# A two-block transformer in one kernel: inverse roots on sums packed into four column tiles, and a convolutional FFN with the gate unit first

## The reference, cut to what matters

```python
def rmsnorm(x, g):                       # rms_norm in the first block is the same
    x32 = x.astype(jnp.float32)
    y = x32 * lax.rsqrt(jnp.mean(x32 * x32, axis=-1, keepdims=True) + RMS_EPS)
    return (y * g.astype(jnp.float32)).astype(x.dtype)

# first block, twice: SEQ 512, D_MODEL 1024; norm, w_in (3584 columns), retention and differential
# attention (rms_norm per head of 64 on dq, dk), w_out; norm, gated FFN (D_FF 2816)

# second block: layer 0 neighbourhood attention (na), layer 1 sliding window (swa);
# layer 0 does the 512 positions and 256 of context, layer 1's FFN the 512 alone
h = modulate(rmsnorm(x, g_attn[i]), sh1, sc1)
q, k, v = attn_inputs(h, w_in, gq, gk, n_kv)               # rmsnorm per head of 64 on q and k
...
def conv_ffn(h, w_up, conv_w, conv_b, w_down):
    t = h.shape[1]
    u = h @ w_up
    u_p = jnp.pad(u, ((0, 0), (CONV_W // 2, CONV_W // 2), (0, 0)))
    u = sum(u_p[:, tap:tap + t] * conv_w[tap] for tap in range(CONV_W)) + conv_b
    a, g = jnp.split(u, 2, axis=-1)
    return (a * jax.nn.silu(g)) @ w_down
```

## Time and profile before

| | before |
|---|---|
| device time, median of 3 runs | 3473.67 us (3472.83 to 3476.34) |
| the profiled execution: its time, its span | 3476.96 us, 3475.2 us |
| PE busy | 3143.3 us (90%), 15176 matmuls |
| DVE busy | 1960.5 us (56%) |
| ACT busy | 1252.3 us (36%) |
| POOL busy | 1072.6 us (31%) |
| chain that ended last | PE 64%, DVE 14%, issue 13%, ACT 4%, POOL 2% |
| L578, main matmuls | 54% of the chain |
| L502, `w_lo` on POOL | 364 of 2618 ns on average |
| L953, `w_hi` on ACT | 364 of 1115 ns on average |
| L1497, head norms' reciprocal | 42, 4038 ns on average |

### The profile page before, as it was taken

How to read it: one execution, slowest core, us unless ns; L and a number is a source line. 1 busy time by engine, 2 the same in 40 slices (tenths; PEclk the granted TensorE clock), 3 DMA queues, 4 the chain that set the end, 5 groups by cost and what they waited for, 6 DMA issues and landing times.

```text
span 3475.2 us, 44398 instructions
## 1 busy us (share of the span) xinstructions
PE 3143.3 (90%) x15176; PEld 2406.6 (69%) x15176; DVE 1960.5 (56%) x2788; ACT 1252.3 (36%) x1801; POOL 1072.6 (31%) x468
## 2 busy tenths in 40 slices
PE   6997689998899679999899988999999798988998
PEld 4752368886672258888687666888888576766777
DVE  5537765455736875455672775552454477566273
ACT  3224444222232535222322762441232226545232
POOL 2320144444330034444223222222223230234343
PEclk9989799999998889999899998999999899999999
DMA  3330034343340024444111001121112120022222
GB/s 132 121 107 0 18 120 149 126 150 102 109 149 0 0 85 145 133 145 133 37 54 58 24 22 48 55 64 63 60 60 67 37 68 13 31 67 85 82 92 92
DMA packets 72775, 269.59 MB, mean 78 GB/s; under 512 B 7920, under 2 KB 8944, under 8 KB 72560
## 3 DMA queue, kind: packets, MB, share of 16 engines
q1 hardware_dynamic: 71024, 264.34, 24.0%
q10 hardware_dynamic: 1664, 4.11, 0.3%
HBM read 266.32 MB, written 2.10 MB: 77 GB/s over the span
## 4 chain that ended last, share of the span: by engine, by line
PE 64%; DVE 14%; issue 13%; ACT 4%; POOL 2%; DVEq 1%; ACTq 0%; DMA 0%; POOLq 0%
PE ps L578 54%; PE ps L668 2%; PE ps L678 2%; DVE conv_y L1588 2%; POOL w_lo L502 2%; DVE conv_y L1584 2%; DVE n_xn L1448 2%; PE ps L725 1%; DVE n_rstd L1435 1%; PE ps L808 1%; PE ps L787 1%; DVE s_s L1864 1%; PE ps L611 1%; PE ps L826 1%; PE ps L634 1%
## 5 line engine op out<-in xcount | busy, mean ns | idle before, releaser
L502 POOL TENSOR_TENSOR w_lo<-w_raw,w_hi 128x1024 fp32r<-128x1024 f32 (+1 forms) x364 | 952.6, 2618 | 1618.7 <-ACT w_hi L953 1618.7
L578 PE MATMUL ps<-h_hi,w_hi 128*128 128x512 f32 x3040 | 1059.1, 383 | 138.9 <-DVE h_lo L1462 84.0
L578 PE MATMUL ps<-h_hi,w_lo 128*128 128x512 f32 x3040 | 1034.9, 375 | 0.0
L578 PE MATMUL ps<-h_lo,w_hi 128*128 128x512 f32 x3040 | 1033.4, 374 | 0.0
L953 ACT ACTIVATE w_hi<-w_raw 128x1024 fp32r<-128x1024 f32 (+1 forms) x364 | 405.6, 1115 | 1091.1 <-PE ps L578 1083.7
L578 PEld LDWEIGHTS ps<-h_hi,w_hi 128*128 128x128 f32 x3040 | 539.6, 192 | 286.7 <-issue 99.9
L578 PEld LDWEIGHTS ps<-h_lo,w_hi 128*128 128x128 f32 x3040 | 537.7, 192 | 102.8 <-issue 6.3
L578 PEld LDWEIGHTS ps<-h_hi,w_lo 128*128 128x128 f32 x3040 | 537.7, 192 | 101.9
L1584 DVE TENSOR_SCALAR conv_y<-u_pad,small 128x770 f32<-128x770 f32 (+1 forms) x88 | 148.0, 1682 | 150.0 <-ACT u_pad L1108 150.0
L1542 DVE SCALAR_TENSOR_TENSOR xT<-ps,mod,xT 128x512 f32 (+1 forms) x72 | 45.4, 659 | 309.7 <-PE ps L578 309.7
L1588 DVE SCALAR_TENSOR_TENSOR conv_y<-u_pad,small,conv_y 128x770 f32<-128x770 f32 (+1 forms) x176 | 195.7, 1112 | 26.2 <-DVE conv_y L1584 6.7
(11 more groups left out here) (187 smaller groups left out, 3649.2 us busy)
## 6 DMA issues: line engine op xcount, KB each, us to landing
mod_w<-w_mod_dram SPq DMA_DIRECT2D x96, 512.0 KB, 3.7
w_raw<-w_gu_dram SPq DMA_DIRECT2D x88, 512.0 KB, 3.6
w_raw<-w_down_dram SPq DMA_DIRECT2D x64, 704.0 KB, 4.1
w_raw<-w_up_dram SPq DMA_DIRECT2D x88, 512.0 KB, 3.6
w_raw<-w_in_dram SPq DMA_DIRECT2D x56, 512.0 KB, 3.7
w_raw<-na_qkv_dram SPq DMA_DIRECT2D x24, 512.0 KB, 3.6
w_raw<-w_out_dram SPq DMA_DIRECT2D x16, 512.0 KB, 3.6
w_raw<-swa_qkv_dram SPq DMA_DIRECT2D x12, 512.0 KB, 3.6
```

The costliest lines, as they stand in the source:

```text
L502: pool.tensor_tensor(w_lo[par][:, 0:cols], w_raw[par][:, 0:cols], w_hi[par][:, 0:cols].bitcast(F32), ALU.subtract).then_inc(w_lo_ready, 1)
L578: last = pe.matmul(acc[par][:, to:to + n], w[par][:, k * P:k * P + P], r[:, k, frm:frm + n], start=begin, stop=end)
```

## The change

**Matrices.** `mats` has ten 128x128 matrices for five. In `PACK`, columns 0 and 1 are 1/64 over the first and the second 64 partitions, and column 32 is 1/1024; the other columns of a tile's 32 are zero. `SPREAD64` and `SPREAD128` have a one where the row of a packed mean meets the partitions that it is for.

**Packed sums.** `groups(T)` divides the columns into four groups: 128 each at T = 512, and windows of 256 at 768. PE multiplies each group into a column tile of 32 partitions of one PSUM bank (`n_packed` in bank 7; `hn_packed` in banks 6 and 7 by parity), by four matmuls with a semaphore increment each where there was one (or two) over the whole array. Root and reciprocal then run over 128 or 256 columns in `n_rs` or `hn_rs`. Four more matmuls over 64 rows each spread the result to 128 partitions and T columns in `sums[0]` (banks 4 and 5), from which DVE's products read it; PE waits for the reciprocal before them. This holds for the eight norms and for the 42 head norms. The norms inside retention and attention (reciprocals at L1698 and L1757, 16 in all) are as before.

**Order in the `normed` phases.** The sum of a unit stands one unit later, and its spreading (`head_cast`) another unit later. The sum and the spreading of the last two units (`tail`) go behind K tiles 2 and 5 of the next phase's first unit; for swa the rotations beside it move by three places (`ROPE_AT`). DVE's loop becomes take, invert, scale, take, invert, scale.

**Conv.** The weights and the taps' table are put in the other order, so that the gate unit comes first. ACT copies a unit once three taps of the parity's previous use are done; Silu follows the taps of both; the product goes to a buffer of its own, `conv_z`. ACT makes the high part of f-1 behind its first copy of f, DVE the low part of f-1 between the two groups of taps. The first pair is peeled on ACT and DVE; the last high and low part stand behind the loop.

The diff, cut to its core:

```diff
+def groups(T):
+    if T == S:
+        return [(g, g * P, P, S * (g // 2) + P * (g % 2), 0, P) for g in (0, 2, 1, 3)]
+    return [(0, 0, 2 * P, 0, 0, 2 * P), (2, S, 2 * P, S, 0, P),
+            (1, 2 * P, 2 * P, 2 * P, 0, 2 * P), (3, S, 2 * P, S + P, P, P)]
...
+            def pack(to, select, square, T, begin=True, end=True):
+                return [pe.matmul(to[32 * g:32 * g + 32, 0:w], mats[:, PACK, select:select + 32],
+                                  square[:, frm:frm + w], start=begin, stop=end) for g, frm, w, _, _, _ in groups(T)]
+            def spread(select, r, T):
+                return [pe.matmul(sums[0][:, to:to + w], mats[g // 2 * HD:g // 2 * HD + HD, select + g % 2, :],
+                                  r[g // 2 * HD:g // 2 * HD + HD, frm:frm + w], start=True, stop=True)
+                        for g, _, _, to, frm, w in groups(T)]
...
             def head_sum(ph, n, par):
                 pe.wait_ge(hn_sq_ready, n + (ph["hn0"] + 1))
-                for to, _, w, _ in segments(ph["T"]):
-                    last = pe.matmul(sums[par][:, to:to + w], mat(MEAN64), hn_sq[par][:, to:to + w],
-                                     start=True, stop=True)
-                last.then_inc(hn_sum, 1)
+                for mm in pack(hn_packed[par], 0, hn_sq[par], ph["T"]):
+                    mm.then_inc(hn_sum, 1)
+
+            def head_cast(ph, n, par):
+
+                pe.wait_ge(hn_recip, n + (ph["hn0"] + 1))
+                if not isinstance(n, int) or n + ph["hn0"] > 0:
+                    pe.wait_ge(hn_out, n + ph["hn0"])
+                for mm in spread(SPREAD64, hn_rs[par], ph["T"]):
+                    mm.then_inc(hn_cast, 1)
...
+                def pair(i):
+                    unit(ph, i, 0, False)
+                    head_sum(ph, i * 2 - 1, 1)
+                    head_cast(ph, i * 2 - 2, 0)
+                    unit(ph, i, 1, False)
+                    head_sum(ph, i * 2, 0)
+                    head_cast(ph, i * 2 - 1, 1)
+
+                if n > 2:
+                    pair(1)
+                    with pe.Fori(2, n // 2) as i:
+                        pair(i)
+
+                def tail(k):
+                    if k == 2:
+                        head_sum(ph, n - 1, 1)
+                        head_cast(ph, n - 2, 0)
+                    if k == 5:
+                        head_cast(ph, n - 1, 1)
+                ends[0] = tail
...
+                    pack(n_packed, 32, n_sum_sq, T, True, False)
                     pe.wait_ge(n_sq_ready, KT * n0 + KT)
-                    add_up(n_sq[1], False, True).then_inc(n_sum, 1)
+                    for mm in pack(n_packed, 32, n_sq[1], T, False, True):
+                        mm.then_inc(n_sum, 1)
+                pe.wait_ge(n_recip, n0 + 1)
+                for mm in spread(SPREAD128, n_rs, T):
+                    mm.then_inc(n_cast, 1)
...
+                def hi(f):
+                    act.wait_ge(conv_step, BEGUN + f * 7 + (7 * n0 + 7))
+                    act.activation(a_hi[:, dyn(f), 0:W], row(conv_z[:, 0:W]), ACT.Copy).then_inc(conv_hi, 1)
+
                 def body(f, split):
+                    first = isinstance(f, int) and f == 0
                     for par in range(2):
                         act.wait_ge(mm_done, f * 2 + (ph["unit0"] + par + 1))
                         split(par)
-                        act.wait_ge(conv_step, BEGUN + f * 7 + 7 * n0)
+                        act.wait_ge(conv_step, BEGUN + 7 * n0 if first else BEGUN + f * 7 + (7 * n0 + 3 * par - 4))
                         for to, frm, n, _ in segments(T, CTX_AT):
                             last = act.activation(u_pad[par][:, 2 + frm:2 + frm + n], acc[par][:, to:to + n], ACT.Copy)
                         last.then_inc(acc_free, 1)
-                    act.wait_ge(conv_step, BEGUN + f * 7 + (7 * n0 + 6))
-                    act.activation(conv_y[1][:, 0:W], conv_y[1][:, 0:W], ACT.Silu).then_inc(conv_gate, 1)
-                    act.wait_ge(conv_step, BEGUN + f * 7 + (7 * n0 + 7))
-                    act.activation(a_hi[:, dyn(f), 0:W], row(conv_y[0][:, 0:W]), ACT.Copy).then_inc(conv_hi, 1)
-                units_of(ph, body)
+                        if par == 0 and not first:
+                            hi(f - 1)
+                    act.wait_ge(conv_step, BEGUN + f * 7 + (7 * n0 + 3))
+                    act.activation(conv_y[0][:, 0:W], conv_y[0][:, 0:W], ACT.Silu).then_inc(conv_gate, 1)
+                units_of(ph, body, peel=1)
+                hi(FH - 1)
...
+                        if T == S:
+                            last = dve.scalar_tensor_tensor(
+                                out=halves(row(n_xn[k % 4][:, 0:S])), in0=halves(row(xT[:, k, 0:S])), scalar=gain,
+                                in1=spread_out(T), op0=ALU.mult, op1=ALU.mult)
...
+                def invert(i, par):
+                    dve.wait_ge(hn_std, i * 2 + (h0 + par + 1))
+                    r = hn_rs[par][:, 0:packed(T)]
+                    dve.reciprocal(r, r).then_inc(hn_recip, 1)
+
                 def scale(i, par):
-                    dve.wait_ge(hn_std, i * 2 + (h0 + par + 1))
-                    dve.reciprocal(hn_r[par][:, 0:T], hn_r[par][:, 0:T]).then_inc(hn_recip, 1)
-                    dve.wait_ge(hn_recip, i * 2 + (h0 + par + 1))
-                    dve.scalar_tensor_tensor(out=tile(i, par), in0=tile(i, par),
+                    dve.wait_ge(hn_cast, i * 8 + 4 * (h0 + par + 1))
+                    dve.scalar_tensor_tensor(out=halves(tile(i, par)), in0=halves(tile(i, par)),
                                              scalar=dcol(ph["gains"][0], i * 2 + (ph["gains"][1] + par)),
...
                         take(i, 0)
+                        invert(i - 1, 1)
+                        scale(i - 1, 0)
+                        take(i, 1)
+                        invert(i, 0)
                         scale(i - 1, 1)
-                        take(i, 1)
-                        scale(i, 0)
-                scale(ph["units"] // 2 - 1, 1)
+                invert(last, 1)
+                scale(last, 0)
+                scale(last, 1)
...
+                def lo(f):
+                    dve.wait_ge(conv_hi, f + (n0 + 1))
+                    dve.tensor_tensor(a_lo[:, bass.ds(f, 1), 0:W], row(conv_z[:, 0:W]),
+                                      a_hi[:, bass.ds(f, 1), 0:W].bitcast(F32), ALU.subtract).then_inc(a_lo_ready, 1)
+
+                def body(f):
+                    taps(f, 0)
+                    if not isinstance(f, int):
+                        lo(f - 1)
+                    taps(f, 1)
                     dve.wait_ge(conv_gate, f + (n0 + 1))
                     dve.wait_ge(conv_step, BEGUN + f * 7 + (m + 6))
-                    dve.tensor_tensor(conv_y[0][:, 0:W], conv_y[0][:, 0:W], conv_y[1][:, 0:W], ALU.mult
+                    dve.wait_ge(a_lo_ready, BEGUN + f + (ph["glu0"] + n0))
+                    dve.tensor_tensor(conv_z[:, 0:W], conv_y[1][:, 0:W], conv_y[0][:, 0:W], ALU.mult
                                       ).then_inc(conv_step, 1)
-                    dve.wait_ge(conv_hi, f + (n0 + 1))
-                    dve.tensor_tensor(a_lo[:, bass.ds(f, 1), 0:W], row(conv_y[0][:, 0:W]),
-                                      a_hi[:, bass.ds(f, 1), 0:W].bitcast(F32), ALU.subtract).then_inc(a_lo_ready, 1)
+
+                body(0)
+                with dve.Fori(1, FH) as f:
+                    body(f)
+                lo(FH - 1)
...
-    up = i["ffn_w_up_2"].reshape(DEPTH, D, 2, FT, P).transpose(0, 1, 3, 2, 4)
+    up = i["ffn_w_up_2"].reshape(DEPTH, D, 2, FT, P).transpose(0, 1, 3, 2, 4)[:, :, :, ::-1]
```

132 lines of the change are left out of this document (70 added, 62 removed).

## The result

| | before | after |
|---|---|---|
| median of the runs | 3475.01 us (3472.83 to 3479.12, 4 runs) | 3372.76 us (3371.78 to 3373.53, 4 runs) |
| ratio, 95% interval | | 0.9698 (0.9686 to 0.971) |
| second measurement, on another occasion | 3476.91 us (9 runs) | 3374.50 us (5 runs), 0.9703 (0.9689 to 0.9716) |
| span of the profiled run | 3475.2 us | 3371.7 us |

A forecast was written before the change was run, and what follows sets the result against it. PE is busy for 90% of the span, but norms, block 1's head norms and layer 1's conv were held by others, chiefly DVE. Savings 33 + 10 + 28 + 6 = 77 us gave 3400 profiled, 3397 median; range 3366 to 3438.

The forecast's parts named there:

- Norms: Eight RMS norms between stages: packing saves 2.9 us each at 512 columns, 6.2 at 768; 33 in all, bounds 18 to 42.
- Head norms: 42 tiles: block 1 saves 21.7 us, na loses 9.7, swa loses 1.6; net 10 saved.
- block 1's 15 and 10 shorter: Sign of being right: block 1's two head-norm stages get shorter by 15 and 10 us.
- Conv loops: Layer 1's conv halves: the loop of product, split, copy and taps falls to 11.0 us a pair; 28 us saved.
- 120 to 123 us: Sign of being right: a conv half of layer 1 takes this long for 528 matmuls.
- Conv at 768 tokens: Conv stages with 768 tokens: said to run at PE's pace already, so no gain was counted.
- Conv ends: Ends of conv halves: 2 us saved per 512 half, 0.9 per 768 half, 6 in all; a wait of 3 stays.
- Rival 3: Four tiles overlap fully and DVE is free beside Pool: 15 and 9 us more, 3373; chance 0.17.
- Rival 1: Packed matmuls run one after the other: 37 us on head norms, 8 on norms, 3442; chance 0.18, whole or in part.
- rival 2: Conv stays a DVE and Pool ring: conv gains 15 us, not 28; 3410; chance 0.15.
- rival 4: Slower: PE waits at every head cast, 3 us more for each of 42 tiles; 3523; chance 0.04.
- Rival 5: The change leaves 16 retention and attention norm reciprocals (L1698, L1757) untouched; number stays, no share of chance.

The follow-up runs named there:

- Experiment 3: Changed kernel, but DVE copies each norm's spread factor from PSUM to SBUF and the eight products read that copy; 3408.06 us, ratio 0.98.
- Experiment 4: Changed kernel with all 42 head norms as in the kernel before; 3383.73 us, ratio 0.9728.
- experiment 5: Changed kernel with all head norms as before, but a stage's last sum inside the next stage's first unit; 3374.58 us, ratio 0.9711.
- experiment 2: Kernel before with only ACT's first conv pair written out ahead of its loop; 3466.02 us (one run).
- experiment 1: Kernel before with the convolution's change alone, no norm changed; 3435.78 us (4 runs), ratio 0.9886.

## Why the prediction was right, and where it was short

- **What bounds the kernel.** Right. Block 1's second head-norm stage and the conv's second half now run with PE busy throughout; these were the places named as held by others.
- **Norms: mechanism right, the term mis-sized.** Root and reciprocal came as worked out; the handoff was 0.84 us where the sum has 1.35. Of the 17 us that the forecast lacks here, 5 are in the steps to the next stage and 12 in the units behind them. The term that failed is "I take 0.7 us a norm at 512 and 3.9 at 768" for products that no longer share with Pool: the first units alone gave 2.1 to 2.4 and 4.9 to 5.8. I had the rows (2.44 beside 1.41, three times a norm) and took most of it back with the argument that the low part would then meet Pool instead. It does not: it stands between Pool's subtractions and takes its usual 0.75, since these became shorter too (1.72 to 1.29 at 512 columns). Experiment 3 gives the whole back. With 50 us this term is also outside the bounds given for it (18 to 42), because their upper end kept the same deduction.
- **Head norms.** Right in the waits and in the loss of na, and partly by luck in the price of a tile: 1.26 us of PE for 1.27 forecast, at 768 a unit of 10.30 for 10.41, 1.82 of it beyond main matmuls at 8.48, for 2.07. The sums took 0.35 and 0.57 us where the sum has 0.59 and 1.06, since they do overlap; the casts took 0.65 and 1.06 for 0.59 and 0.85, and the changes of form around them more than the 0.1 that I gave them. Experiment 4 shows that na's loss is the packed head norms'. What I had not separated is the moved tail: experiment 5 puts 3.5 of 11 in a stage on it, and over the kernel it makes the whole net gain. The sign "block 1's 15 and 10 shorter" does not follow from my own sum (11.7 and 10.0, once the 4 us for set-up are in); measured were 10.5 and 11.4.
- **Conv loops.** Right: 10.88 us a pair for 11.0, because the ring has dropped below PE's pace. The split between table loads (12.9) and the rest (7.0 and 8.7) is experiment 2's. The sign "120 to 123 us" held for the second half (119.7); the first took 124.0, with its own norm's waits in its first unit.
- **Conv at 768 tokens.** "Run at PE's pace" was right and still no reason for zero: PE's own pace has two values. This is the second miss, 3.5 to 7 us. The one profile of before shows both values: na's plain units at 66.69 / 8 = 8.34 us in the earlier trace rows, the first conv half's at 178.09 / 21 = 8.48. What it can't show is which of them an execution takes.
- **Conv ends.** 5.5 for 6; the wait was 2.46 us where 3 were forecast.
- **Rivals.** Rival 3's number (3373) came true, and both halves of its mechanism are in the traces: DVE is free beside Pool, and the tiles overlap. But the number came by luck: the overlap gave none of its 15 us, because a tile still costs 1.26 us, and the norms gave 17 us more than forecast where this rival has 9. Rival 1 is refuted by the 1.26 us a tile, rival 2 by 119.71 us, rival 4 by the idle time of 0.0 ahead of the casts' 264 records. Rival 5 was as said: those 16 reciprocals are unchanged and in no term.

## What to carry to other kernels

When a VectorE operation with two SBUF inputs stands in line with GpSimd, look for a form in which one input is in PSUM, and read the price from the maximum of its durations, not from the median; do not take the gain back on an argument for which no row stands. Packing a reduction's result to fewer columns pays where VectorE is late, and costs where TensorE is the bound (na): decide it stage by stage. Before a rearrangement is credited with a gain, try its smallest part alone: here one peeled pair gave 12.9 us, and a sum moved into the next stage a third of the head norms' gain in block 1 and, over the kernel, all of their net gain.

## What the hardware showed that I had not expected

- Two paces of the same matmuls: 48 matmuls of 512 and 256 columns in 8.32 or in 8.48 us, at full granted clock, changing from execution to execution in one stage; 3.5 us for a stage of 22 units, and less in shorter ones. The runs of experiment 1 spread over some 7 us (3432.5 to 3440.3); that the paces are the reason is not shown, since one of the four was profiled.
- Four passes on four column tiles start within 21 ns and take 0.11 to 0.13 us together, as long as one; two on two row halves likewise. Half of a packed head norm's 1.26 us on PE is not passes but the change between forms, some 0.2 us each time.
- With two SBUF inputs both sides lose at 512 columns: Pool's subtraction in the norm takes 1.72 us beside such products (in the kernel before and in experiment 3) and 1.29 without them. At 768 columns it takes 1.83 us either way, and DVE's products alone lose.
